# Hybrid decoder step on one core: the prompt's head norm moved into the samples' memory stage, and the samples' states loaded one stage earlier

## The chip, the cores and the metric

One Trainium2 chip, one of its cores. The metric is the device time of one execution in microseconds (us); lower is better. The profile has five engines: PE (TensorE; PEld is its weight load), DVE (VectorE), ACT (ScalarE), POOL (GpSimd) and SP (SyncE), from whose queue all DMAs here are issued.

## The reference, cut to what matters

One layer of a decoder runs on a prompt of 512 tokens (with 16 learned tokens ahead of it) and on 8 samples of 4 new tokens each. An input projection feeds 8 heads of differential attention and 4 heads of mLSTM, a matrix memory. Each head's output is normed, and the norms of all heads go into one output projection:

```
def rms_norm(x, g):
    y = xf * lax.rsqrt(jnp.mean(xf * xf, axis=-1, keepdims=True) + EPS)
    return (y * g.astype(jnp.float32)).astype(x.dtype)
...
    hn = rms_norm(h, g)                                  # mLSTM heads, 256 wide
    o = jax.nn.sigmoid(og.astype(jnp.float32)).reshape(B, T, N_HEADS_M, HEAD_DIM_M)
    return (hn * o).reshape(B, T, MLSTM_WIDTH)
...
    a = (rms_norm(a_heads, attn_out_norm) * (1.0 - lam_init)).reshape(B, T, ATT_WIDTH)
    x = x + jnp.concatenate([a, m_out], axis=-1) @ w_out
    hf = rms_norm(x, norm_ffn) @ w_up
    return x + jnp.square(jax.nn.relu(hf)) @ w_down
```

In an mLSTM head of a sample, the state C (256 by 256 for each of 8 samples and 4 heads, 8.4 MB together) is read from memory, used (`num = w_inter * (q @ C0) + s @ v`), updated (`C = w_c * C0 + k^T v`) and written back. The prompt's mLSTM begins with a state of zero.

## The kernel before, in words

The kernel is a row of stages. Each is a block in which the five engines run their own instruction lists and meet through semaphores; at its end all engines meet, and a second small block clears the stage's semaphores. So no work of one stage overlaps the next. The order is: input projection, attention of the prompt (`heads_and_attention`), conv and features (`mlstm_features`), the prompt's memory (`prompt_mlstm`), the samples' memory (`sample_mlstm`), attention of the samples over the paged cache (`decode_attention`), output projection (`finish_and_project`), MLP, output. All heads' outputs lie in one SBUF tensor, `mix` (128 partitions by 16 chunks of 128 features by 560 tokens: 528 of the prompt with the learned ones, then 32 of the samples).

`prompt_mlstm` loops over 4 heads with two sets of buffers. SP loads heads 0 and 1 (9 DMAs each, 2.5 MB, `load`, L1068), and then for each head waits for its state, stores it (L1087) and its normaliser (L1089: 256 elements of 4 bytes, each a run of its own), waits until the head's last output is placed and loads head h+2 into the freed buffers.

`sample_mlstm` first issues on SP, head by head, 7 small loads (L1277) and 8 loads of states (L1289, 256 KB each). TensorE does for each head h: `sums(h)` (L1426, 16 matmuls with the states of the 8 samples; the profile counts 32, since a float32 matmul shows as two instructions), one more for the new tokens (L1429), and then 16 outer products (L1458) into four PSUM banks in turn, which VectorE adds into the state one by one (L1379). VectorE also divides the head's output (`divide`, after `sums`), and prepares the next head in the middle of its additions (`weigh(h + 1)`). SP stores each new state as it is made (L1301). ScalarE is all but idle.

`finish_and_project` norms the heads and projects them. VectorE squares 16 chunks of 544 tokens (L2167), TensorE sums the squares over the partitions with one-hot weights (`gather`, L2231), ScalarE takes the sigmoid of the output gates `og` (L2119) and VectorE multiplies them in (L2173); then root (ScalarE, L2124) and reciprocal (VectorE, L2183) of all heads together; TensorE spreads the 12 rows of inverse roots over the partitions (`scatter`, L2241), and VectorE multiplies each chunk by it and the gain (L2194). ScalarE rounds the chunk to float32r (`mix_hi`, L2127) and VectorE makes the remainder (`mix_lo`, L2187). The weights of `w_out` come in 16 tiles of 1 MB and are split in the same way (L2094 on ScalarE, `leading`; L2139 on VectorE, `trailing`). A tile is 96 matmuls: two halves of 272 tokens, 16 chunks k, 3 passes (`exact_passes`, L69 to L71). Into the first tile's first half TensorE waits chunk by chunk for `mix_lo`. When all of `mix_lo` is made, `mix` is overwritten with the residual by one DMA of 4.35 MB (L2067), to which VectorE adds each tile's result (L2145). TensorE may begin tile n when tile n-2 has been added.

## Time and profile before

| | us |
|---|---|
| median of 3 runs | 3865.28 |
| lowest, highest | 3864.36, 3869.47 |
| the profiled execution: its time | 3864.66 |
| the same: its span | 3862.6 |
| TensorE busy | 3595.9 (93% of the span) |
| VectorE busy | 1808.7 (47%) |
| ScalarE busy | 1280.9 (33%) |
| the prompt's memory stage | 935.30 to 1042.37 |
| the samples' memory stage | 1042.37 to 1149.72 |
| output projection, before its first matmul with `w_out` | 2014.80 to 2080.80 |
| output projection, from there to its last matmul | 2080.80 to 2274.7 |

A stage begins with its first instruction or DMA issue. The busy share of TensorE is high in the projections and the MLP, and says little of the stages in this table: in the 66 us before the first matmul with `w_out` it is busy 37 us. Since all engines meet between stages, a stage counts with its own length.

### The profile page before, as it was taken

The numbers are of one execution on the slowest core, as the hardware profiler recorded it, in microseconds if no ns is written. First come the engines' busy times: TensorE is split into PE (matmuls) and PEld (weight loads), VectorE is DVE, ScalarE is ACT, GpSimd is POOL, SyncE is SP. The second block draws the span as 40 slices with busy tenths as digits, with TensorE's granted clock in tenths as the row PEclk, the third lists the DMA queues.
The fourth block names the chain that finished last, engine by engine and source line by source line (L and its number), as shares of the span: only waits on it lengthen the run. The fifth ranks groups of instructions, "written<-read, shape, count | busy, mean of one in ns | idle before, by whom it ended". The sixth has DMA issues, their size and how long they took to land. (4 is left out here: it accounts for less than half of the span.)

```text
span 3862.6 us, 65521 instructions
## 1 busy us (share of the span) xinstructions
PE 3595.9 (93%) x26234; PEld 3328.7 (86%) x26234; DVE 1808.7 (47%) x2749; ACT 1280.9 (33%) x1879; POOL 713.8 (18%) x436
## 2 busy tenths in 40 slices
PE   7999998866789999999977999999999999999998
PEld 7999996545658888888846999999999999999998
DVE  4222223764447777777765343333333333333333
ACT  3111111432107777777752232222222222222221
POOL 0000000000005888888870000000000000000000
PEclk9999999768869999999988999999999999999999
DMA  7443332115548899999964322222222222222221
GB/s 206 111 111 106 105 107 87 51 53 170 115 152 315 319 327 328 331 326 329 327 210 124 87 75 88 88 88 88 88 88 88 88 88 88 88 88 88 88 88 58
DMA packets 454169, 564.77 MB, mean 146 GB/s; under 512 B 39462, under 2 KB 330196, under 8 KB 453388
## 3 DMA queue, kind: packets, MB, share of 16 engines
q1 hardware_dynamic: 453932, 561.47, 45.3%
q8 instruction: 166, 2.72, 0.3%
q14 instruction: 71, 0.58, 0.0%
HBM read 514.93 MB, written 46.47 MB: 145 GB/s over the span
## 5 line engine op out<-in xcount | busy, mean ns | idle before, releaser
L1599 POOL TENSOR_TENSOR dc_vl<-dc_vpages,dc_vh 128x1024 fp32r<-128x1024 f32 x256 | 609.0, 2395 | 19.0 <-ACT dc_vh L1928 18.6
L69 PE MATMUL f_acc<-hidden_hi,ffn_lo 128*128 128x272 f32 x2048 | 591.7, 289 | 2.8 <-DVE mix_t L2353 2.8
L71 PE MATMUL f_acc<-xf_hi,ffn_hi 128*128 128x272 f32 x2048 | 594.1, 290 | 0.0
L71 PE MATMUL f_acc<-hidden_hi,ffn_hi 128*128 128x272 f32 x2048 | 592.9, 290 | 0.0
L69 PE MATMUL f_acc<-xf_hi,ffn_lo 128*128 128x272 f32 x2048 | 591.0, 289 | 1.0 <-DVE xf_lo L2375 0.4
L70 PE MATMUL f_acc<-hidden_lo,ffn_hi 128*128 128x272 f32 x2048 | 590.7, 288 | 0.0
L70 PE MATMUL f_acc<-xf_lo,ffn_hi 128*128 128x272 f32 x2048 | 588.5, 287 | 0.0
L69 PE MATMUL z_acc<-xn_hi,win_lo 128*128 128x280 f32 x1536 | 447.6, 291 | 1.1 <-DVE win_lo L302 1.1
L71 PE MATMUL z_acc<-xn_hi,win_hi 128*128 128x280 f32 x1536 | 448.5, 292 | 0.0
L2304 ACT ACTIVATE ffn_hi<-ffn_raw 128x2048 fp32r<-128x2048 f32 x127 | 242.3, 1908 | 619.4 <-PE f_acc L71 619.4
L70 PE MATMUL z_acc<-xn_lo,win_hi 128*128 128x280 f32 x1536 | 447.3, 291 | 0.0
L1770 DVE TENSOR_TENSOR dc_kl<-dc_pk,dc_kh 128x512 fp32r<-128x512 f32 x512 | 337.7, 681 | 151.9 <-ACT dc_kh L1928 151.4
L69 PEld LDWEIGHTS f_acc<-hidden_hi,ffn_lo 128*128 128x128 f32 x2048 | 384.5, 188 | 6.4 <-DVE mix_t L2353 6.4
L69 PEld LDWEIGHTS f_acc<-xf_hi,ffn_lo 128*128 128x128 f32 x2048 | 385.7, 188 | 4.3 <-DVE xf_lo L2375 3.6
L70 PEld LDWEIGHTS f_acc<-xf_lo,ffn_hi 128*128 128x128 f32 x2048 | 386.6, 189 | 0.0
L70 PEld LDWEIGHTS f_acc<-hidden_lo,ffn_hi 128*128 128x128 f32 x2048 | 386.0, 188 | 0.0
L71 PEld LDWEIGHTS f_acc<-xf_hi,ffn_hi 128*128 128x128 f32 x2048 | 385.4, 188 | 0.0
L71 PEld LDWEIGHTS f_acc<-hidden_hi,ffn_hi 128*128 128x128 f32 x2048 | 384.9, 188 | 0.0
L2358 DVE TENSOR_TENSOR ffn_lo<-ffn_raw,ffn_hi 128x2048 fp32r<-128x2048 f32 x127 | 291.2, 2293 | 150.8 <-ACT ffn_hi L2304 150.8
L2353 DVE TENSOR_TENSOR mix_t<-mix_t,f_acc 128x544 f32<-128x544 f32 x256 | 182.9, 720 | 362.1 <-PE f_acc L71 362.1
L1928 ACT ACTIVATE dc_kh<-dc_pk 128x512 fp32r<-128x512 f32 x512 | 278.4, 596 | 127.3 <-PE dc_pk L1627 126.3
L69 PEld LDWEIGHTS z_acc<-xn_hi,win_lo 128*128 128x128 f32 x1536 | 289.4, 188 | 1.3 <-DVE win_lo L302 1.3
(359 smaller groups left out, 6248.8 us busy)
## 6 DMA issues: line engine op xcount, KB each, us to landing
dc_kpages<-in_cache_k SPq DMA_DIRECT2D x256, 512.0 KB, 5.4
dc_vpages<-in_cache_v SPq DMA_DIRECT2D x256, 512.0 KB, 5.2
ffn_raw<-in_w_up SPq DMA_DIRECT2D x64, 1024.0 KB, 6.4
ffn_raw<-in_w_down SPq DMA_DIRECT2D x64, 1024.0 KB, 5.0
win_raw<-in_w_in SPq DMA_DIRECT2D x48, 1024.0 KB, 6.1
ffn_raw<-in_w_out SPq DMA_DIRECT2D x16, 1024.0 KB, 6.3
z_scratch<-z_out SPq DMA_DIRECT2D x48, 280.0 KB, 2.4
sm_c<-in_state_C SPq DMA_DIRECT2D x32, 256.0 KB, 4.5
```

What stands on the lines that cost most here:

```text
L69: nc.tensor.matmul(out, wlo, xhi, start=first, stop=False)
L70: nc.tensor.matmul(out, whi, xlo, start=False, stop=False)
L71: return nc.tensor.matmul(out, whi, xhi, start=False, stop=last)
L1599: G.tensor_tensor(vl[:, m % VBUF, :], vring[:, m % RING, :], vh[:, m % VBUF, :].bitcast(F32), ALU.subtract).then_inc(vlo, 1)
L1770: V.tensor_tensor(kl[:, k, hs, i * P:(i + 1) * P], pk[i][half][:, :].rearrange("p (h t) -> p h t", h=HH), kh[:, k, hs, i * P:(i + 1) * P]. ...
L1928: A = lambda out, x, **more: nc.scalar.activation(out, x, ACT.Copy, **more)
L2304: nc.scalar.activation(flow.hi[:, i % 2, :], flow.raw[:, i % G, :], ACT.Copy).then_inc(flow.hi_made, 1)
L2353: nc.vector.tensor_tensor(halves(xt[:, oc, :]), halves(xt[:, oc, :]), acc[2 + i % 2][:, :, 0:d.ohalf], ALU.add).then_inc(added, 1)
L2358: nc.vector.tensor_tensor(flow.lo[:, i % 2, :], flow.raw[:, i % G, :], flow.hi[:, i % 2, :].bitcast(F32), ALU.subtract).then_inc(flow.lo_m ...
```

## The change

Three things are done together.

- **States.** The buffers of the samples' states and their semaphores are made before `prompt_mlstm` (class `Early`, in a stage of its own around both), and the 32 loads of states are issued there, on SP, behind the loads of heads 0 and 1 and ahead of the first store.
- **Head norm of the prompt.** The norm and the output gate of the 512 prompt tokens move from `finish_and_project` into `sample_mlstm`: squares on ScalarE and 8 sums of squares (512 columns each) on TensorE behind each of the first two heads' outer products; behind head 1 the root, the reciprocal and the four gates; the 12 rows of inverse roots go to DRAM and come back as 12 broadcast loads, queued on SP behind the stores of head 1; behind head 2 VectorE multiplies 16 chunks. `num` has one PSUM bank in place of two, and the other is `mean`.
- **Output stage.** Only the 32 sample tokens are normed there, in one instruction where there were 16. The `w_out` tile 0 is loaded first. Both halves of `mix_hi` and `mix_lo` are made separately (`columns`): half 0 is all prompt tokens and its first 8 chunks are split at once, half 1 after the samples' norm. The residual comes in four DMAs, each when four chunks of half 1 have been split.

The functions not shown below are as before. The core of the diff:

```diff
+    def __init__(self, nc, ctx, d, sems):
+        self.states = [ctx.enter_context(nc.sbuf_tensor(f"sm_c0{h}", [P, d.nb, d.md // P, d.md + 1], F32))
+                       for h in range(d.hm)]
+        self.states_in = [sems(f"sm_c_in{h}") for h in range(d.hm)]
...
             for h in range(d.hm):
+                for b in range(d.nb):
+                    sp.dma_start(early.states[h][:, b, :, 0:d.md], a["state_C"][0, b, h].rearrange(
+                        "(e p) n -> p e n", p=P)).then_inc(early.states_in[h], 16)
...
         score = ps("sm_score", [P, 512])
-        num = [ps(f"sm_num{i}", [P, 512]) for i in range(2)]
+        num = ps("sm_num", [P, 512])
+        mean = ps("ph_mean", [P, 512])
...
             sp.dma_start(nrows[:, :], a["state_n"][0].rearrange("b h n -> (b h) n")).then_inc(states_in, 16)
             for h in range(d.hm):
                 load(sp, h)
-                load_states(sp, h)
+            for i in range(d.hm):
+                sp.dma_start(og[i][:, :, :], ogv[cog // E + i][:, :, N_META:TP]).then_inc(og_in[i], 16)
...
                                  c0[h][:, b, :, 0:MD]).then_inc(stored, 16)
+                if h == 1:
+                    sp.wait_ge(inv_made, 1)
+                    sp.dma_start(inv_dram, inv[:, :]).then_inc(inv_out, 16)
+                    sp.wait_ge(inv_out, 16)
+                    for i in range(NH):
...
+                dve.wait_ge(sigmoid_made, h + 1)
+                dve.wait_ge(squared, d.ha + (h + 1) * E)
+                x = prompt[:, d.ha + h * E:d.ha + (h + 1) * E, :]
+                V.tensor_tensor(x, x, og[h][:, :, :], ALU.mult).then_inc(gated, 1)
+            def invert():
+                dve.wait_ge(gathered, d.kc)
+                V.tensor_scalar(root[:, :], mean[0:NH, 0:S], EPS, None, ALU.add).then_inc(rooting, 1)
+                dve.wait_ge(rooted, 1)
...
+                    V.tensor_scalar(gains[:, 0:1], gains[:, 0:1], 1.0 - LAM_INIT, None, ALU.mult).then_inc(gated, 1)
+                    dve.wait_ge(gated, d.hm + 1)
+                gain = gains[:, 0:1] if n < d.ha else gains[:, 1 + (n - d.ha) % E:2 + (n - d.ha) % E]
+                V.scalar_tensor_tensor(prompt[:, n, :], prompt[:, n, :], gain, spread[:, head(n), :],
+                                       ALU.mult, ALU.mult).then_inc(normed, 1)
             for s in range(d.hm):
...
+                if h == 1:
+                    invert()
+                    for i in range(d.hm):
+                        gate(i)
                 dve.wait_ge(state_new, E * NB * (h + 1))
                 V.tensor_copy(nbh(ncols[:, :, :])[:, :, :, h], c0[h][:, :, :, MD]).then_inc(new_put, 1)
+                if h == d.hm - 2:
+                    for n in range(d.kc):
+                        norm(n)
             for e in range(E):
                 dve.wait_ge(new_turned, e + 1)
...
+                for n in part(h):
+                    if n >= 8:
+                        act.wait_ge(gathered, n - 7)
+                    nc.scalar.activation(sq[n % 8][:, :], prompt[:, n, :], ACT.Square).then_inc(squared, 1)
                 act.wait_ge(summed, h + 1)
...
                     raise_weights(h + 1)
+                if h == 1:
+                    for i in range(d.hm):
+                        act.wait_ge(og_in[i], 16)
+                        nc.scalar.activation(og[i][:, :, :], og[i][:, :, :], ACT.Sigmoid).then_inc(sigmoid_made, 1)
+                    act.wait_ge(rooting, 1)
+                    nc.scalar.activation(root[:, :], root[:, :], ACT.Sqrt).then_inc(rooted, 1)
...
                 pe.wait_ge(states_put, h + 2)
-                if h >= 2:
-                    pe.wait_ge(divided, h - 1)
+                if h:
...
                         scores(h + 1)
+                for n in part(h):
+                    pe.wait_ge(squared, n + 1)
+                    pe.wait_ge(gather_made, 3)
+                    x = head(n)
+                    nc.tensor.matmul(mean[0:NH, 0:S], gather[:, int(n >= d.ha), NH - 1 - x:2 * NH - 1 - x], sq[n % 8][:, :],
+                                     start=(n == 0), stop=(n == d.kc - 1)).then_inc(gathered, 1)
             pe.wait_ge(new_put, d.hm)
...
         def _(sp):
+            sp.dma_start(tile(flow.raw, 0), w[:, :, 0:P]).then_inc(flow.landed[0], 16)
+            sp.dma_start(og[:, :, :], ogv[:, :, d.tp:d.t]).then_inc(og_in, 16)
...
                 sp.dma_start(tile(flow.raw, j), w[:, :, j * P:(j + 1) * P]).then_inc(flow.landed[j], 16)
-            for h in range(2, d.hm):
-                sp.wait_ge(gated, (h - 1) * E)
-                sp.dma_start(og[:, h % 2, :, :], ogv[cog // E + h][:, :, N_META:d.t]).then_inc(og_in[h % 2], 16)
-            sp.wait_ge(lo_made, d.kc)
-            sp.dma_start(xt[:, :, :], x_dram.rearrange("(k p) t -> p k t", p=P)[:, :, N_META:d.t]).then_inc(residual_in, 16)
+            x = x_dram.rearrange("(k p) t -> p k t", p=P)[:, :, N_META:d.t]
+            for i in range(4):
+                rows = slice(i * QUAD, (i + 1) * QUAD)
+                sp.wait_ge(lo_made, N + (i + 1) * QUAD)
+                sp.dma_start(xt[:, rows, :], x[:, rows, :]).then_inc(residual_in, 16)
             with sp.Fori(0, N // GROUP - 1) as g:
...
-                act.wait_ge(og_in[h % 2], 16 * (h // 2 + 1))
-                nc.scalar.activation(og[:, h % 2, :, :], og[:, h % 2, :, :], ACT.Sigmoid).then_inc(sigmoid_made, 1)
...
+            for n in range(N // 2):
+                split(0, n)
+            act.wait_ge(og_in, 16)
...
             nc.scalar.activation(root[:, :], root[:, :], ACT.Sqrt).then_inc(rooted, 1)
-            for n in range(d.kc):
-                act.wait_ge(scaled, n + 1)
-                nc.scalar.activation(mhi[:, n, :], mix[:, n, :], ACT.Copy).then_inc(hi_made, 1)
+            act.wait_ge(flow.landed[0], 16)
+            leading(0)
+            for n in range(N // 2, N):
+                split(0, n)
+            act.wait_ge(scaled, 3)
+            for n in range(N):
+                split(1, n)
+                if n == N // 2:
+                    act.wait_ge(flow.landed[1], 16)
...
-                    dve.wait_ge(sigmoid_made, h + 1)
-                    dve.wait_ge(squared, i + 1)
-                    x = mix[:, d.ha + h * E:d.ha + (h + 1) * E, :]
-                    V.tensor_tensor(x, x, og[:, h % 2, :, :], ALU.mult).then_inc(gated, E)
-                if i in (9, 11):
-                    trailing(dve, (i - 9) // 2, (i - 9) // 2)
+            V.tensor_tensor(ssq[:, :, :], smp, smp, ALU.mult).then_inc(squared, 1)
...
+                trail(0, n)
             dve.wait_ge(gains_in, 32)
             V.tensor_scalar(gains[:, 0:1], gains[:, 0:1], 1.0 - LAM_INIT, None, ALU.mult).then_inc(gated, 1)
-            dve.wait_ge(gated, d.hm * E + 1)
-            dve.wait_ge(summed, d.kc)
-            V.tensor_scalar(two(root[:, :]), mean[0:NH, :, 0:d.ohalf], EPS, None, ALU.add).then_inc(rooting, 1)
+            dve.wait_ge(summed, 1)
+            V.tensor_scalar(root[:, :], means[0:NH, 0:TS], EPS, None, ALU.add).then_inc(rooting, 1)
+            dve.wait_ge(sigmoid_made, 1)
+            V.tensor_tensor(smp[:, d.ha:N, :], smp[:, d.ha:N, :], og[:, :, :], ALU.mult).then_inc(gated, 1)
...
-            def trail(n):
-                dve.wait_ge(hi_made, n + 1)
...
-                dve.wait_ge(spread_ready, h + 1)
-                V.scalar_tensor_tensor(two(mix[:, n, :]), two(mix[:, n, :]), gain, spread[h % 2][:, :, 0:d.ohalf],
+            V.reciprocal(inv[:, :], root[:, :]).then_inc(inverted, 1)
+            trailing(dve, 0, 0)
+            dve.wait_ge(gated, 2)
+            dve.wait_ge(spread_ready, 1)
+            rows = lambda lo, hi: spread[:, lo * TS:hi * TS].rearrange("p (h t) -> p h t", t=TS)
+            V.scalar_tensor_tensor(smp[:, 0:d.ha, :], smp[:, 0:d.ha, :], gains[:, 0:1], rows(0, d.ha),
+                                   ALU.mult, ALU.mult).then_inc(scaled, 1)
+            heads_m = smp[:, d.ha:N, :].rearrange("p (h e) t -> p e h t", e=E)
+            for e in range(E):
+                V.scalar_tensor_tensor(heads_m[:, e], heads_m[:, e], gains[:, 1 + e:2 + e], rows(d.ha, NH),
                                        ALU.mult, ALU.mult).then_inc(scaled, 1)
-                if n >= 1:
-                    trail(n - 1)
-            trail(d.kc - 1)
+            for n in range(N // 2, N):
+                trail(0, n)
+            for n in range(N):
+                trail(1, n)
+                if n == N // 2:
+                    trailing(dve, 1, 1)
             dve_group(dve, 0, True)
             with dve.Fori(1, N // GROUP) as g:
...
         def _(pe):
-            pe.wait_ge(consts, 6)
-            for i in range(d.kc):
-                n = d.ha + i if i < d.kc - d.ha else i - (d.kc - d.ha)
-                h = head(n)
-                pe.wait_ge(squared, i + 1)
-                for b in range(2):
-                    mm = nc.tensor.matmul(mean[0:NH, b, 0:d.ohalf], gather[:, int(n >= d.ha), NH - 1 - h:2 * NH - 1 - h],
-                                          sq[i % 2][:, b * d.ohalf:(b + 1) * d.ohalf], start=(i == 0),
-                                          stop=(i == d.kc - 1))
-                mm.then_inc(summed, 1)
+            pe.wait_ge(consts, 5)
+            pe.wait_ge(squared, 1)
+            for n in range(N):
+                x = head(n)
+                mm = nc.tensor.matmul(means[0:NH, 0:TS], gather[:, int(n >= d.ha), NH - 1 - x:2 * NH - 1 - x],
+                                      ssq[:, n, :], start=(n == 0), stop=(n == N - 1))
+            mm.then_inc(summed, 1)
             pe.wait_ge(inverted, 1)
             for h in range(NH):
-                if h >= 2:
-                    pe.wait_ge(scaled, h - 1 if h - 2 < d.ha else d.ha + (h - 1 - d.ha) * E)
-                for b in range(2):
-                    mm = nc.tensor.matmul(spread[h % 2][:, b, 0:d.ohalf], scatter[:, h, :],
-                                          inv[:, b * d.ohalf:(b + 1) * d.ohalf], start=True, stop=True)
...
-                sample_mlstm(nc, d, a, sems, c, qk_dram, kt_dram, vt_dram, g_dram, mix, c_sample, n_sample)
+            with ExitStack() as two, stage(nc) as early_sems:
+                early = Early(nc, two, d, early_sems)
+                with stage(nc) as sems:
+                    prompt_mlstm(nc, d, a, sems, c, qk_dram, kt_dram, vt_dram, g_dram, mix, c_prompt, n_prompt, early)
+                with stage(nc) as sems:
+                    sample_mlstm(nc, d, a, sems, c, z_dram, qk_dram, kt_dram, vt_dram, g_dram, inv_dram, mix, c_sample,
```

## Rows read from the trace of the kernel before

**Rows 1.** The page: its first line.
```profile
span 3862.6 us, 65521 instructions
```

**Rows 2.** Windows, output stage: length, PE, PEld, DVE, ACT, POOL, PEclk, DMA share, GB/s.
```profile
2014.80:2080.80 66.00, 37.16 (x112) 16.45 (x113) 41.34 (x51) 19.54 (x22) 3.76 (x6) 0.78 0.35 98
...
2094.00:2274.70 180.70, 180.70 (x1439) 180.55 (x1437) 54.67 (x45) 36.98 (x30) 0.00 (x0) 1.00 0.38 104
```

**Rows 3.** Timeline of that stage, PE and ACT: start us, us, what.
```profile
2080.80 0.81 PE L69 MATMUL o_acc<-mix_hi,ffn_lo 128*128 128x272 f32 x1
...
2093.92 1.92 ACT L2094 ACTIVATE ffn_hi<-ffn_raw 128x2048 fp32r<-128x2048 f32 x1 [8.76 <-PE o_acc L71]
```

**Rows 4.** Groups of instructions by line, the same stage.
```profile
L2194 DVE SCALAR_TENSOR_TENSOR mix_t<-mix_t,fh_gains,fh_spread 128x544 f32<-128x544 f32 x16 | 12.4, 775 | 3.3 <-PE fh_spread L2241 3.3
...
L2183 DVE RECIPROCAL fh_inv<-fh_root 12x544 f32<-12x544 f32 x1 | 3.5, 3541 | 0.7 <-ACT fh_root L2124 0.7
...
L2139 DVE TENSOR_TENSOR ffn_lo<-ffn_raw,ffn_hi 128x2048 fp32r<-128x2048 f32 x16 | 36.7, 2292 | 6.6 <-ACT ffn_hi L2094 6.6
...
L2094 ACT ACTIVATE ffn_hi<-ffn_raw 128x2048 fp32r<-128x2048 f32 x16 | 30.7, 1918 | 134.9 <-PE o_acc L71 129.0 <-DMA ffn_raw<-in_w_out 5.9
...
L2127 ACT ACTIVATE mix_hi<-mix_t 128x544 fp32r<-128x544 f32 x16 | 10.5, 658 | 17.2 <-DVE mix_t L2194 17.2
```

**Rows 5.** Timeline of ScalarE, the same stage: one table load.
```profile
2040.58 1.28 ACT L2124 ACT_TABLE_LOAD   x1
```

**Rows 6.** DMA issues: KB each, us to landing (second: 1042.3 to 1046).
```profile
ffn_raw<-in_w_out SPq DMA_DIRECT2D x16, 1024.0 KB, 6.3
...
sm_qk<-qk_scratch SPq DMA_DIRECT2D x1, 64.0 KB, 2.0
```

**Rows 7.** Timeline of VectorE at the first addition of the residual.
```profile
2099.51 0.72 DVE L2145 TENSOR_TENSOR mix_t<-mix_t,o_acc 128x544 f32<-128x544 f32 x1 [13.59 <-DMA mix_t<-xt_scratch]
```

**Rows 8.** Timeline of TensorE in the samples' memory stage.
```profile
1047.66 0.42 PE L1413 MATMUL sm_score<-sm_qk 128*32 128x32 f32 x4 [2.55 <-DMA sm_src<-g_scratch]
...
1056.17 9.73 PE L1426 MATMUL sm_num<-sm_c,sm_qpad 128*32 128x257 f32 x32 [8.08 <-DMA sm_c<-in_state_C]
...
1078.59 8.79 PE L1426 MATMUL sm_num<-sm_c,sm_qpad 128*32 128x257 f32 x32
...
1100.08 9.97 PE L1426 MATMUL sm_num<-sm_c,sm_qpad 128*32 128x257 f32 x32
```

**Rows 9.** Windows of the same stage, columns as in Rows 2.
```profile
1056.20:1061.50 5.30, 5.30 (x13) 2.23 (x14) 0.00 (x0) 0.00 (x0) 0.00 (x0) 0.50 1.06 337
...
1071.90:1082.00 10.10, 8.22 (x19) 4.23 (x18) 6.10 (x19) 0.00 (x0) 0.00 (x0) 0.50 1.00 325
```

**Rows 10.** Timeline of TensorE: the sums of squares of the output stage.
```profile
2052.03 3.91 PE L2231 MATMUL fh_spread<-fh_sq,fh_gather 128*12 128x272 f32 x16 [1.47 <-DVE fh_sq L2167]
```

**Rows 11.** Timeline of the prompt's memory stage: SP's queue, then VectorE.
```profile
967.38 0.47 SPq L1089 DMA_DIRECT2D out<-ml_state  x1
...
971.49 0.37 SPq L1068 DMA_DIRECT2D ml_qk<-qk_scratch  x1
...
993.08 1.51 DVE L1194 TENSOR_SCALAR ml_w<-ml_negtop,ml_src 112x528 f32<-112x528 f32 x5
```

**Rows 12.** Windows of the prompt's stage; the last is of the samples'.
```profile
936.00:954.50 18.50, 7.71 (x23) 5.16 (x24) 4.54 (x14) 2.69 (x7) 0.00 (x0) 0.56 1.02 289
...
972.00:978.00 6.00, 4.68 (x29) 3.49 (x27) 5.61 (x18) 2.27 (x7) 0.00 (x0) 1.00 0.74 44
...
978.00:988.00 10.00, 9.89 (x68) 8.97 (x67) 6.60 (x19) 0.92 (x3) 0.00 (x0) 1.00 1.01 242
...
1058.00:1061.00 3.00, 3.00 (x9) 1.23 (x8) 0.00 (x0) 0.00 (x0) 0.00 (x0) 0.50 1.06 365
```

**Rows 13.** Timeline at a stage boundary: last instruction, first of the next.
```profile
2011.70 0.20 ACT L1928 ACTIVATE mix_t<-dc_pscore 128x32 f32<-128x32 f32 x1 [13.18 <-PE dc_pscore L1720]
...
2014.80 0.34 SPq L2055 DMA_DIRECT2D fh_gains<-in_attn_out_norm  x1
```

128 lines of the change are left out of this document (76 added, 52 removed).

## The prediction

> **What bounds the kernel now.** I read the page first: the span is 3862.6 us [rows 1]. Since all engines meet between stages, no average over the span prices this change; three stretches do. The windows of the output stage give the first: 66.0 us pass before its first matmul with `w_out`, with TensorE busy 37 of them and VectorE 41, neither full [rows 2]. The PE timeline dates that matmul at 2080.80 [rows 3]. From there TensorE is busy all the time: 180.7 us after 2094.0, 0.1256 us per matmul, so 12.06 for a tile of 96. The first tile ends at 2093.92, where ScalarE is released [rows 3]. Second, the samples' memory stage: TensorE idles 8.08 us for the states' DMA before `sums(0)`, then the heads follow each other 22.4 and 21.5 us apart, with 8.8 to 10 us of `sums` in each, in which VectorE has nothing [rows 8]. Third, the prompt's memory stage hides its loads, and the question there is by how much.
>
> **Output stage.** Removed: squares, gates, reciprocal over 544 columns, and 16 chunk norms with their splits, ahead of the projection. What releases the first matmul now is the weights' split behind the samples' norm. From the stage's start at 2014.80:
> - `w_out` tile 0, issued first, lands after about 6.3 us, as such tiles do [rows 6]: 2021.1. The samples' gates are issued next, 1024 runs of 128 bytes; 512 such runs landed 2.0 us after issue on a free queue [rows 6], so about a microsecond behind the tile: 2022.0. ScalarE's eight first splits are done by then (272 columns, half of 0.66 us each or a little more [rows 4], 3 us).
> - ScalarE: the table load for the sigmoid (1.28 [rows 5]) fits before 2022.0; sigmoid of 256 columns 0.4, table load for the root 1.28, root 0.2, then `leading(0)` 1.92 [rows 4]: 2025.8.
> - VectorE: `trailing(0)` 2.29 [rows 4]: 2028.1. TensorE starts there instead of at 2080.80.
>
> TensorE will have done only 28 small matmul pairs before and starts at the half clock. In the samples' stage a burst after idling ran at 0.50 for 5.3 us [rows 9]; that much at half clock costs 2.65 us. VectorE must keep ahead: after 2028.1 three small products (1.0), then 24 half-chunk remainders of about 0.38 with `trailing(1)` (2.29) between. It finishes chunk 9 of half 1 at 2038.5, and TensorE reaches it at 2028.1 + 2.65 + 6.03 + 3.4 = 2040.2; after that both go at 0.38. No stall, by 1.7 us. So tile 0 ends at 2028.1 + 12.06 + 2.65 = 2042.8 instead of 2093.92: **-51.1 us**. The residual (4.35 MB, 13.6 us with its wait before [rows 7]) is now asked for from about 2034 to 2041 in quarters and is there by 2048; then addition 0.72 and `trailing(2)` 2.29, 2051, and TensorE wants tile 2 at 2042.8 + 12.06 = 2054.9. Hidden, by 4 us. Bounds: everything at its earliest (gates together with the tile, warm clock) -54.5; gates landing 4 us later and 3 us of stalls -44.
>
> **Samples' memory stage.** (a) With the states there, `sums(0)` follows the scores at 1047.66 + 0.42, say 1048.3 instead of 1056.17 [rows 8]: -7.9. (b) 8 sums of squares behind head 0's outer products. TensorE executes in order, so `sums(1)` comes after them, and VectorE has nothing to do meanwhile: all of it is on the path. At full clock 16 instructions of 272 columns took 3.91 [rows 10], so 512 columns are 0.46 each and 16 of them 7.4; at half clock 14.8. The stretch in which they start ran at 0.50 until 1082.0 [rows 9], 3.4 us into them: I take 3.4 + 16 x 0.46 - 1.7 = 9.0. `sums(1)` then runs at full clock, 16 pairs of 257 columns, 32 x 0.23 (0.244 x 257/272) = 7.4 where it took 8.79: net +7.6. (c) The same behind head 1, 7.4 to 9, take 8.0; but here VectorE's chain to head 2 decides: root's addition 0.7, root 0.66, reciprocal 3.3 (3.54 for 544 columns), four gates of 1024 columns at 1.2 (half of a 2048-column remainder [rows 4]) 4.8, hand-overs 0.3: 9.8 behind the last sum, against 9.97 + 0.8 for `sums(2)` and its division before [rows 8]: 8.0 + 9.8 - 10.8 = +7.0. (d) Sixteen norms of 512 columns, 775 x 512/544 = 730 ns [rows 4], 11.7 with 0.4 around, beside `sums(3)` of about 10 and 0.6: +1.5. Their inputs: the inverse roots leave some 4.8 us after the last sum, are in DRAM 2 us later, 12 issues of 0.5 follow, and 3 MB need 11 us at 289 GB/s [rows 12]: 18 to 20 us, where VectorE wants them after 9.8 + 13 = 23. Squares (5 us), sigmoids and table loads lie on an idle ScalarE; one bank for `num` costs nothing, since `divide` is over 12 us before the next `sums`. Sum: **+8.2 us**. Bounds: +4 (both groups at full clock, norms under `sums(3)`) and +20 (both at half clock).
>
> **Prompt's memory stage.** The 32 state loads are issued on SP in 16 us from 948.6, behind the first 5.3 MB, which end at 954.5 at 289 GB/s [rows 12]. State loads alone ran at 365 GB/s [rows 12]: 8.4 MB take 23.0 us, to 977.5. Queued behind them are the first store of the state, the 4-byte store of the normaliser, and the load of head 2. Before, that store was issued at 967.38 and the load at 971.49 [rows 11], and though nothing else was in the queue the load crawled at 44 GB/s from 972 to 978 and went at 242 only then [rows 12]: the small store holds the queue for some 10 us. Head 2 is wanted at 993.08 [rows 11], and the load was in by about 991 to 992 (the window 978 to 988 moved 2.4 of its 2.5 MB, the rest trickled), so 1 to 2 us are spare. If the store now begins at 978 instead of 967.9, everything behind it moves by 10, and head 2 starts 8 to 9 us late; load 3 suffers the same shift and adds 1. I take **+9**. Below: if store and states overlap in the queue, the 2.5 MB land by 988 and nothing is lost: 0. Above: states at 289 GB/s, +14.
>
> [...]
>
> **Boundary.** `Early` has a block of its own that clears 4 semaphores. Two such blocks and their meetings took 2014.80 - 2011.90 = 2.9 us [rows 13]; one more, nearly empty: **+1** (0.5 to 1.5). Decoding, MLP and output keep their work.
>
> **Sum.** -51.1 + 8.2 + 9 + 1 = -32.9. The profiled execution (3864.66, 2.1 above its span) becomes 3831.8; the median is 0.6 above it, so 3832.
>
> **The rivals.**
> - *States hidden.* The prompt's stage keeps its length. For it: the states' bytes fit into the empty queue between 954.5 and 978. Against: the crawl. -42, 3823.
> - *TensorE's extra sums at half clock and late broadcasts.* For it: half of the samples' stage ran at 0.50. Samples +20, prompt +12: -18, 3847.
> - *Output stage gives back.* The four residual DMAs queue ahead of `w_out` tile 4 and behind each other, or VectorE's splits keep TensorE waiting in half 1: up to 10 us more, -23, 3842. Against: 4 and 1.7 us of margin above, though the latter is small.
> - *Slower: the broadcasts.* Each of 12 loads reads one row of 2 KB 128 times. If such loads go one after another at the 44 GB/s of the crawl rather than at 289, 3 MB take 70 us, 50 more than is free; norm 0 waits and with it VectorE and the fourth head: +17, 3882. It decides from 60 us for the twelve, 5 us each. Against: the first 5.3 MB held four broadcasts and ran at 289 GB/s overall [rows 12].
>
> **How the numbers follow.** Forecast (within 5 us of 3832) 0.45, hidden states 0.17, half clock 0.18, output stage gives back 0.14, broadcasts 0.04, something else that costs 30 us 0.02. The range 3819 to 3851 leaves out 1 in 10 below and above together with the slower cases; the forecast's own range is 3826 to 3839. 0.2% (7.7 us) is about what a measurement of this kernel can tell from no change. Faster holds the first four cases, 0.94; within 0.2% the last, 0.02; slower the broadcasts, 0.04.
>
> **What would show it.** First matmul with `w_out` 13 to 14 us after its stage's first issue (66 before); half clock in its first 5 us; no wait of tile 2. In the samples' stage `sums(0)` 6 us after the stage's start, its length up by 8.2 (the 7.9 of waiting already taken off); VectorE's first norm not waiting for a DMA. In the prompt's stage, VectorE waiting some 9 us for `ml_src` ahead of head 2. The prediction is wrong if that wait is absent, if the sums of squares run at half clock throughout, or if VectorE waits for `ph_spread`.

## The result

The changed kernel took 3833.8 us (median of 4 runs, 3826.6 to 3834.7) beside 3865.2 for the kernel before (4 runs, 3864.4 to 3869.5): a ratio of 0.9913, 95% interval 0.9901 to 0.9925. Forecast were 3832 and a range of 3819 to 3851. A later set with the same kernel gave 3834.6 (5 runs) and 0.9921 (0.9908 to 0.9935).

The profiled execution took 3832.93 us. The first line of its page, which answers to [rows 1]:

```profile
span 3831.2 us, 65582 instructions
```

All engines meet between stages, so the difference of the two spans, -31.4, can be booked stage by stage. A stage runs from SP's first DMA issue in it to the first of the next stage; the output stage is cut where ScalarE is released by the end of tile 0.

| | before | after | moved | forecast |
|---|---|---|---|---|
| all before the prompt's memory stage | 935.30 | 933.88 | -1.4 | 0 |
| prompt's memory stage | 107.07 | 114.45 | +7.4 | +9 |
| samples' memory stage | 107.35 | 117.71 | +10.4 | +8.2, and +1 for the block |
| decoding | 865.08 | 869.41 | +4.3 | 0 |
| output stage up to the end of tile 0 | 79.12 | 28.09 | -51.0 | -51.1 |
| the rest | 1768.68 | 1767.66 | -1.0 | 0 |

**Output stage.** Windows of the kernel after (columns as in [rows 2]): from the first issue to the first matmul with `w_out`, then tile 0, then the tiles behind it.

```profile
2035.45:2049.79 14.34, 7.13 (x56) 6.90 (x56) 8.43 (x15) 10.24 (x21) 3.45 (x5) 0.50 0.96 242
2049.79:2063.54 13.75, 13.75 (x100) 13.75 (x100) 11.65 (x28) 7.04 (x18) 0.00 (x0) 0.89 0.78 237
2063.54:2243.00 179.46, 179.46 (x1431) 179.46 (x1430) 54.67 (x45) 37.05 (x30) 0.00 (x0) 1.00 0.39 105
```

14.34 us pass instead of 66.0, tile 0 has no gap in it, and behind it TensorE is busy for all of 179.46 us, at 0.1254 us per matmul: nothing is given back. What stands on the way to the first matmul is shown by the timelines of ScalarE, VectorE and TensorE in the kernel after:

```profile
2042.15 0.42 ACT L2212 ACTIVATE fh_og<-fh_og 128x256 f32<-128x256 f32 x1 [2.71 <-DMA fh_og<-z_scratch]
...
2044.02 1.89 ACT L2183 ACTIVATE ffn_hi<-ffn_raw 128x2048 fp32r<-128x2048 f32 x1
...
2063.54 1.92 ACT L2183 ACTIVATE ffn_hi<-ffn_raw 128x2048 fp32r<-128x2048 f32 x1 [5.48 <-PE o_acc L71]
...
2075.59 1.92 ACT L2183 ACTIVATE ffn_hi<-ffn_raw 128x2048 fp32r<-128x2048 f32 x1 [4.06 <-PE o_acc L71]
```
```profile
2045.94 2.29 DVE L2236 TENSOR_TENSOR ffn_lo<-ffn_raw,ffn_hi 128x2048 fp32r<-128x2048 f32 x1 [1.46 <-ACT ffn_hi L2183]
```
```profile
2044.54 5.33 PE L2330 MATMUL fh_spread<-fh_inv,fh_scatter 12*128 12x32 f32 x24 [3.44 <-DVE fh_inv L2276]
2049.79 0.59 PE L69 MATMUL o_acc<-mix_hi,ffn_lo 128*128 128x272 f32 x1
```

The weights' remainder (`trailing(0)`, L2236) is done at 2048.23, 12.8 us after the stage's start; the forecast had 13.3. But TensorE starts only at 2049.79. Its 24 small products with `fh_scatter`, which run at the half clock of the first window (0.50), end no earlier. So the last thing to end is another instruction than in the forecast, 1.6 us behind it. Tile 0 ends at 2063.54 and the next at 2075.59, 12.05 later, so tile 2 does not wait. The residual comes late, as the timeline of VectorE shows (kernel after), but it is hidden: the addition and `trailing(2)` behind it are done at 2073.04, 2.5 us before TensorE wants tile 2 (the forecast had 4).

```profile
2070.11 0.72 DVE L2242 TENSOR_TENSOR mix_t<-mix_t,o_acc 128x544 f32<-128x544 f32 x1 [8.47 <-DMA mix_t<-xt_scratch]
```

**Samples' memory stage.** The timeline of TensorE, kernel after; rows of `sm_num<-sm_c` answer to [rows 8], those of L1550 are the sums of squares:

```profile
1053.65 0.42 PE L1495 MATMUL sm_score<-sm_qk 128*32 128x32 f32 x4 [2.31 <-DMA sm_src<-g_scratch]
1054.37 9.60 PE L1508 MATMUL sm_num<-sm_c,sm_qpad 128*32 128x257 f32 x32 [0.30 <-DVE sm_c L1376]
...
1076.66 8.63 PE L1550 MATMUL ph_mean<-ph_sq,ph_gather 128*12 128x512 f32 x16
1085.12 7.12 PE L1508 MATMUL sm_num<-sm_c,sm_qpad 128*32 128x257 f32 x32
...
1104.93 9.84 PE L1550 MATMUL ph_mean<-ph_sq,ph_gather 128*12 128x512 f32 x16
1114.62 7.12 PE L1508 MATMUL sm_num<-sm_c,sm_qpad 128*32 128x257 f32 x32
...
1135.67 9.91 PE L1508 MATMUL sm_num<-sm_c,sm_qpad 128*32 128x257 f32 x32
...
1148.54 10.62 PE L1540 MATMUL sm_acc<-sm_v,sm_kw 32*128 32x257 f32 x24
```

The wait of 8.08 us for the states is gone: `sums(0)` starts 6.04 us after the stage's first issue (1048.33) where it started 13.80 after. From there the heads follow each other at 30.75, 29.50 and 21.05 us, where they were 22.4, 21.5 and 24.4 apart: +8.3, +8.0, -3.4 at the starts of `sums`. By the divisions, with which VectorE takes up each head (16.4, 44.7, 75.7 and 98.8 us after the stage's start, where it was 24.3, 45.8, 68.5 and 92.6), it is +6.8, +8.3 and -1.0. The last row matters for the account: head 3's 24 outer products took 10.62 us, and 7.35 in the timeline of the kernel before:

```profile
1136.63 7.35 PE L1458 MATMUL sm_acc<-sm_v,sm_kw 32*128 32x257 f32 x24
```

The timeline of VectorE between the last sum of squares and head 2's division, and at the norms:

```profile
1114.82 0.68 DVE L1412 TENSOR_SCALAR ph_root<-ph_mean 12x512 f32<-12x512 f32 x1 [9.29 <-PE ph_mean L1550]
1116.19 3.34 DVE L1414 RECIPROCAL ph_inv<-ph_root 12x512 f32<-12x512 f32 x1 [0.69 <-ACT ph_root L1486]
1119.46 4.55 DVE L1408 TENSOR_TENSOR mix_t<-mix_t,ph_og 128x1024 f32<-128x1024 f32 x4
...
1124.38 0.47 DVE L1397 TENSOR_SCALAR sm_out<-sm_num,sm_mag 32x256 f32<-32x256 f32 x1
...
1136.57 10.69 DVE L1423 SCALAR_TENSOR_TENSOR mix_t<-mix_t,ph_gains,ph_spread 128x512 f32<-128x512 f32 x16
```

The chain of 9.8 us that was forecast behind the last sum (from 1114.77) took 9.25 to the division's first instruction at 1124.02. The norms begin at 1136.57 without a wait: the twelve broadcasts, issued from 1121.09 to 1127.26, were there.

**Prompt's memory stage.** SP's queue, then VectorE and TensorE at head 2, in the timeline of the kernel after; these answer to [rows 11]:

```profile
947.27 25.82 SPq L1096 DMA_DIRECT2D sm_c<-in_state_C  x32
973.13 0.66 SPq L1101 DMA_DIRECT2D out<-ml_state  x1
973.84 0.67 SPq L1103 DMA_DIRECT2D out<-ml_state  x1
974.55 0.66 SPq L1078 DMA_DIRECT2D ml_qk<-qk_scratch  x1
```
```profile
996.39 1.53 DVE L1208 TENSOR_SCALAR ml_w<-ml_negtop,ml_src 112x528 f32<-112x528 f32 x5 [4.95 <-DMA ml_src<-g_scratch]
```
```profile
996.41 5.88 PE L1125 MATMUL ml_score<-ml_qk 128*112 128x264 f32 x12 [6.63 <-DMA ml_src<-g_scratch]
```

The windows of the same stretch (to set beside [rows 12]):

```profile
972.00:978.00 6.00, 5.27 (x38) 4.66 (x39) 5.61 (x16) 0.55 (x3) 0.00 (x0) 1.00 1.09 349
978.00:984.00 6.00, 6.00 (x47) 5.63 (x46) 4.86 (x15) 0.53 (x2) 0.00 (x0) 1.00 1.06 186
984.00:990.00 6.00, 5.79 (x42) 5.32 (x40) 0.09 (x1) 0.95 (x3) 0.00 (x0) 1.00 1.01 217
```

The crawl of the kernel before (44 GB/s from 972 to 978) does not come back here: the states move at 349 GB/s until 978, and the load behind them at 186 and 217. VectorE waits 4.95 us for `ml_src` before head 2, TensorE 6.63. And TensorE, which had idled for these 6.63 us, computes head 2's first scores in 5.88 us. The same products took 3.37 in the timeline of the kernel before:

```profile
991.34 3.37 PE L1111 MATMUL ml_score<-ml_qk 128*112 128x264 f32 x12
```

The granted clock was 1.00 under that row, and 0.50 from 993.0 to 999.0 and 0.64 from there to 1002.3 in the kernel after. The wait and these slower products (the cold start, below) make the stage longer. The forecast had a wait of 8 to 9 us and no cold start.

### The profile page after: what moved, and what is told of

It is laid out like the page before. It is cut to its first block and busy times, and to the rows that moved or that the text cites. A ratio compares the mean times of both kernels' runs of the same rounds, so it can differ in the third digit from the quotient of the medians.

```text
span 3831.2 us, 65582 instructions
## 1 busy us (share of the span) xinstructions
PE 3588.0 (94%) x26210; PEld 3326.5 (87%) x26210; DVE 1801.5 (47%) x2757; ACT 1293.2 (34%) x1916; POOL 713.4 (19%) x438
```

## The experiments

All twelve were timed beside the kernel before on the same chip. e1 to e4 came in one set, e5 to e8 in a second, f1 to f4 in a third; the kernel before took 3863.7, 3864.9 and 3865.2 us in them. The ratio, which is formed within a set, is the safer figure for a comparison across sets.

| kernel | median us (runs) | ratio, 95% interval | prompt's / samples' / decoding | head 3's outer products |
|---|---|---|---|---|
| before (first profile) | 3865.2 (4) | | 107.1 / 107.4 / 865.1 | 7.35 |
| after (first profile) | 3833.8 (4) | 0.9913 [0.9901, 0.9925] | 114.5 / 117.7 / 869.4 | 10.62 |
| e1 | 3864.7 (10) | 1.0004 [0.9994, 1.0014] | 114.9 / 97.3 / 868.3 | 8.23 |
| e2 | 3831.9 (4) | 0.9919 [0.9902, 0.9935] | 106.8 / 124.1 / 866.6 | 8.12 |
| e3 | 3827.1 (4) | 0.9907 [0.9891, 0.9924] | 111.8 / 114.7 / 866.5 | 7.96 |
| e4 | 3823.1 (4) | 0.9892 [0.9875, 0.9908] | 106.6 / 116.9 / 870.9 | 9.68 |
| e5 | 3825.5 (4) | 0.9896 [0.9879, 0.9912] | 114.9 / 111.1 / 868.8 | 9.12 |
| e6 | 3828.5 (4) | 0.9905 [0.9889, 0.9922] | 114.8 / 116.4 / 866.2 | 10.02 |
| e7 | 3830.7 (4) | 0.9915 [0.9898, 0.9931] | 114.5 / 115.9 / 867.9 | 8.03 |
| e8 | 3824.0 (4) | 0.9894 [0.9878, 0.9911] | 106.9 / 115.2 / 869.2 | 10.61 |
| f1, the changed kernel again | 3834.6 (5) | 0.9921 [0.9908, 0.9935] | 115.1 / 114.6 / 866.5 | 8.01 |
| f4, e4 again | 3824.2 (4) | 0.9895 [0.9880, 0.9911] | 106.9 / 116.2 / 868.1 | 8.05 |
| f2 | 3849.3 (5) | 0.9953 [0.9940, 0.9967] | 107.7 / 139.8 / 868.0 | 10.61 |
| f3 | 3866.8 (1) | | 107.9 / 105.4 / 868.0 | 8.30 |

The three stage lengths are differences of first issues in each kernel's timeline; the last column is its row for the outer products of head 3.

**e1: the early states alone.** The kernel before, plus class `Early` and the 32 loads behind the loads of heads 0 and 1; nothing else of the change.

```diff
+            for h in range(d.hm):
+                for b in range(d.nb):
+                    sp.dma_start(early.states[h][:, b, :, 0:d.md], a["state_C"][0, b, h].rearrange(
+                        "(e p) n -> p e n", p=P)).then_inc(early.states_in[h], 16)
...
-                load_states(sp, h)
```

> The kernel before, with one part of the change alone: the 32 loads of states are issued in the prompt's memory stage behind the first two heads' loads. Theory A (the small 4-byte store and the loads behind the states arrive late, and the third head waits): the prompt's stage is 7 us longer, the samples' stage 8 us shorter by its wait for states and 1 us longer by the extra block; in total 3865 plus 0, within 2 us. Rival B (the states are hidden in an empty queue): the prompt's stage keeps its 107.1 us, and the kernel takes 3858.

The time did not move (1.0004). The prompt's stage is 7.9 us longer and the samples' 10.0 shorter. Of these 10.0, 7.8 are the wait for the states. The rest lies in the later heads, where the same code also differs by 2 us between two executions (107.4 in before, 105.4 in f3). The timeline of VectorE in e1 has the wait in its new place:

```profile
998.23 1.53 DVE L1207 TENSOR_SCALAR ml_w<-ml_negtop,ml_src 112x528 f32<-112x528 f32 x5 [6.31 <-DMA ml_src<-g_scratch]
```

So in this kernel the early loads only carry the wait from one stage into another.

**e2: the change without the early states.** Its loads issued in `sample_mlstm` again, behind each head's small loads.

```diff
-            for h in range(d.hm):
-                for b in range(d.nb):
-                    sp.dma_start(early.states[h][:, b, :, 0:d.md], ...
...
             for h in range(d.hm):
                 load(sp, h)
+                for b in range(NB):
+                    sp.dma_start(c0[h][:, b, :, 0:MD], a["state_C"][0, b, h].rearrange(
+                        "(e p) n -> p e n", p=P)).then_inc(c_in[h], 16)
```

> The changed kernel with the loads of states back in the samples' stage, each head's 8 behind its 7 small loads; all else is kept. Theory A: the prompt's stage falls back from 114.5 to 107.1 us, and the samples' first product with the states starts 13.8 us after the stage's start instead of 6.0, so that the two cancel: 3833 to 3835, as the changed kernel. Rival B (the early loads are worth their 8 us of waiting): 3841.

3831.9, as quick as the change. The prompt's stage has its old length (106.8), and the samples' is 6.3 us longer than in the first profile of after, 9.4 longer than in f1. The whole gain of the change is that of the moved norm together with the new order of the output stage (`w_out` tile 0 first, halves split apart, residual in quarters). No run takes these two from each other.

**e3: the small store behind the next load.** In the changed kernel the store of the normaliser (L1103, 256 values of 4 bytes, two for each partition) goes behind the load of head h+2.

```diff
-                sp.dma_start(n_prompt[0, 0, h].rearrange("(e p) -> p e", p=P), state[s][:, :, d.md],
-                             allow_slow_non_contiguous=True).then_inc(stored[s], 16)
                 if h + 2 < d.hm:
                     sp.wait_ge(placed, NT * (h + 1))
                     load(sp, h + 2, s)
+                sp.dma_start(n_prompt[0, 0, h].rearrange("(e p) -> p e", p=P), state[s][:, :, d.md],
+                             allow_slow_non_contiguous=True).then_inc(stored[s], 16)
```

> The changed kernel with one order changed on SP's queue: in the prompt's stage the store of the normaliser (256 runs of 4 bytes) is issued behind the load of head h+2 instead of ahead of it. The bytes stay the same. Theory A (the small store holds the queue some 10 us, behind the states): the third head waits 2 us at most instead of 5, its matmuls keep the full clock, and the prompt's stage is 5 to 7 us shorter than in the changed kernel: 3827. Rival B (it is the bytes of the states alone that delay the load): the load's landing does not move, and the time is that of the changed kernel, 3833.

The timeline of VectorE in e3 at head 2:

```profile
992.75 1.52 DVE L1208 TENSOR_SCALAR ml_w<-ml_negtop,ml_src 112x528 f32<-112x528 f32 x5 [2.45 <-DMA ml_src<-g_scratch]
```

The wait is 2.45 us instead of 4.95, and the stage 2.6 to 3.2 shorter than in the two profiles of after. So the small store's place accounts for half of the wait. The other half goes only when the states' loads go (e2 and e4). The median of 3827.1 lies lower by more than that, but the interval of its ratio overlaps that of the change, and only the 2.5 us are tied to a row.

**e4 and f4: only head 0's states early.** The other 24 loads go out in the samples' stage, behind each head's small loads.

```diff
-            for h in range(d.hm):
+            for h in range(1):
                 for b in range(d.nb):
                     sp.dma_start(early.states[h][:, b, :, 0:d.md], ...
```

> The changed kernel with only head 0's 8 loads of states (2.1 MB) early; the other 24 are issued in the samples' stage, behind each head's small loads. Theory A: 2.1 MB are through 6 us after the first heads' loads, before the first store is issued; the prompt's stage falls back to 107.1 us, and the samples' first product still starts 6 us after the stage's start: 7 us less than the changed kernel, 3826. Rival B (24 loads, 6.3 MB, in the samples' stage delay head 1, or push the output gates and stores behind them): head 1 waits, and the gain is under 3 us.

> Only head 0's eight state loads early, once more, beside the changed kernel in the same set: 8 us less than it (3824 to 3825) by the theory; under 5 us less by the rival.

SP's queue in e4's timeline:

```profile
947.47 7.20 SPq L1096 DMA_DIRECT2D sm_c<-in_state_C  x8
965.57 0.38 SPq L1101 DMA_DIRECT2D out<-ml_state  x1
```

Eight loads leave SP in 7.20 us, and the first store waits for its data, not for the queue. No engine waits for a DMA at head 2, the prompt's stage takes 106.6 and 106.9 us, and `sums(0)` still starts 6.0 and 7.6 us after the samples' stage begins; `sums(1)` follows the sums of squares without a wait, so heads 1 to 3 need no earlier load. 3823.1 and 3824.2: the best version of the study, measured twice. In the third set it stands beside the changed kernel, 3824.2 against 3834.6.

**f1: the changed kernel again.**

> The changed kernel itself, unchanged, timed beside the next two. Theory: the 8 to 10 us by which the version with only head 0's states early was quicker are the wait and the cold start at head 2 of the prompt's memory stage, so this one gives 3832 to 3834 and that one 3823 to 3825 in the same set. Rival: part of the difference lay between chips; then they stand less than 5 us apart. Decoding, whose code is the same in all kernels, has taken 865.1 to 870.9 us so far; the theory that this is variation from run to run expects a figure in that range that need not be the 869.4 of the first profile, the rival that the change itself made it longer expects 869 again.

3834.6, and 10.4 us behind f4 in the same set (9.0 by the means): the difference is not one between chips. The profiles show 8.1 in the prompt's stage (115.05 against 106.93). They can't book the rest: the profiled execution of f1 is the fastest of its five (3826.8, the others 3834.5 and more), and it lies only 4.3 us above that of f4. Decoding took 866.5 here and 869.4 in the first profile of the same kernel. Over the 14 traces, whose code there is the same, it ranges from 865.1 to 870.9 with a mean of 867.8, and it falls into no order by kernel; the first profile of before has the lowest of them. The +4.3 of the account is therefore most likely chance in one pair of executions. So is most of the 3.3 us at head 3: its outer products take 8.01 here, 10.62 there.

**e5: fewer sums of squares.** Seven of the eight matmul pairs behind head 0's outer products are left out, so the means lack these sums. The first pair waits for all eight squares and reports for all eight.

```diff
                 for n in part(h):
+                    if 1 <= n < 8:
+                        continue
...
```

> The changed kernel without seven of the eight matmuls (14 of 16 instructions) that sum the squares behind head 0: the means of attention heads 1 to 7 lack their sums. Theory A (they stand on the path, since VectorE has nothing to do meanwhile and sums(1) is queued behind them): 14 instructions of 0.46 to 0.9 us go, and sums(1) falls back to a partly half clock: 5 to 7 us less than the changed kernel, 3828. Rival B (TensorE has slack there, or the clock gives it all back): within 2 us of the changed kernel.

The group takes 1.88 us in place of 8.6 (first profile) or 8.4 (f1). The samples' stage is 111.1 us and the time 3825.5. In the timeline `sums(1)` starts 30.21 us after the stage's start instead of 36.79 (first profile) or 36.17 (f1): the group lies on the path with its whole length. Seven pairs gave back 6.0 to 6.6 us, 0.9 us a pair, and nothing covers them.

**e6: the gates on GpSimd.** The four products with the sigmoids leave VectorE's chain to head 2.

```diff
-                V.tensor_tensor(x, x, og[h][:, :, :], ALU.mult).then_inc(gated, 1)
+                nc.gpsimd.tensor_tensor(x, x, og[h][:, :, :], ALU.mult).then_inc(gated, 1)
```

> The changed kernel with the four gate products of the prompt on GpSimd instead of VectorE. Theory A (VectorE's chain behind head 1 is 1.4 us longer than sums(2), so the gates are nearly all covered): divide(2) comes 1.4 us earlier, and the kernel gains 1 to 1.5 us: 3832. Rival B (the whole 4.6 us of the gates are on the path): 3829. Rival C (GpSimd and VectorE slow each other, or GpSimd is too late for the norms): slower than the changed kernel.

GpSimd needs 9.26 us for what VectorE did in 4.55, but it does them while the sums of squares run:

```profile
1100.72 9.26 POOL L1367 TENSOR_TENSOR mix_t<-mix_t,ph_og 128x1024 f32<-128x1024 f32 x4 [51.93 <-ACT ph_og L1485]
```

Head 2's `sm_out` follows the last sum by 8.1 us instead of 9.6. The limit is then TensorE's `sums(2)` (7.12) with the magnitude and the division behind it, so that 1.5 of the 4.55 us come out. The interval of the ratio doesn't set it apart from the change.

**e7: the output stage in another order.** The samples' gates loaded ahead of `w_out` tile 0, sigmoid and root ahead of ScalarE's eight splits, VectorE's eight remainders behind the reciprocal, the means ahead of the wait for `fh_scatter`. The first parts of the edit:

```diff
-            sp.dma_start(tile(flow.raw, 0), w[:, :, 0:P]).then_inc(flow.landed[0], 16)
             sp.dma_start(og[:, :, :], ogv[:, :, d.tp:d.t]).then_inc(og_in, 16)
+            sp.dma_start(tile(flow.raw, 0), w[:, :, 0:P]).then_inc(flow.landed[0], 16)
...
-            for n in range(N // 2):
-                split(0, n)
             act.wait_ge(og_in, 16)
...
+            for n in range(N // 2):
+                split(0, n)
...
```

> The changed kernel with another order at the start of the output stage: the samples' gates are loaded ahead of the first tile of w_out, their sigmoid and root come ahead of the eight splits, and the sums of squares wait only for the gather weights, not for the scatter weights too. Theory A (the first matmul with w_out waits for TensorE's own 12 small spreading matmuls, which run at half clock for 5.3 us because the inverse root is late): it starts 11.2 us after the stage's start instead of 14.3, and the kernel gains 3 us: 3830. Rival B (the tile's landing and its split on ScalarE and VectorE set the start): it starts later than now, since the tile is asked for later, and nothing is gained.

The gates land after 2.4 us instead of 6.2, and the sigmoid starts 2.5 us after the stage's first issue instead of 6.7. Yet the first matmul with `w_out` comes 14.50 us after that issue, no earlier than in the changed kernel (14.34 and 14.49 in its two profiles). The timelines of VectorE and TensorE in e7 say what took the place of the wait:

```profile
2040.67 0.15 DVE L2268 TENSOR_SCALAR fh_gains<-fh_gains 128x1 f32<-128x1 f32 x1 [6.02 <-DMA fh_gains<-in_mlstm_out_norm]
```
```profile
2047.91 0.60 PE L69 MATMUL o_acc<-mix_hi,ffn_lo 128*128 128x272 f32 x1 [0.98 <-DVE ffn_lo L2236]
```

The addition to `fh_root` is queued behind the first of these instructions, which waits for 1.5 KB of gains until 7.3 us after the first issue. ScalarE's eight splits now lie between the root and `leading(0)`. TensorE waits 0.98 us for VectorE's remainder of the weights at the end, where it was its own small products that ended last. Moving one of these chains brought up another, and nothing was gained.

**e8: e4, e6 and e7 together.**

> The changed kernel with three edits together: only head 0's states early, the gates on GpSimd, and the new order in the output stage. If all three theories hold, the gains add: 7 + 1.4 + 3 = 11 us less than the changed kernel, 3822. If they overlap in the clock or the queue, 5 to 8 us.

3824.0, the same as e4. Its profile has the 106.9 of the prompt's stage; what e6 and e7 were hoped to add does not show. It would be within what decoding and head 3's outer products (10.61) vary by.

**f2: operands exchanged.** On top of e4 the squares are the weights and one column of 1/width passes through. The means lie with tokens on the partitions, and root and reciprocal work on 48 columns.

```diff
-                    nc.tensor.matmul(mean[0:NH, 0:S], gather[:, int(n >= d.ha), NH - 1 - x:2 * NH - 1 - x], sq[n % 8][:, :],
-                                     start=(n == 0), stop=(n == d.kc - 1)).then_inc(gathered, 1)
+                            mm = nc.tensor.matmul(mean[:, x * J + j:x * J + j + 1], sq[n % 8][:, j * P:(j + 1) * P],
+                                                  gather[:, int(n >= d.ha), NH - 1:NH],
+                                                  start=(n == chunks[0]), stop=(n == chunks[-1]))
```

> Head 0's states alone early, and the sums of squares with the operands exchanged: the squares are the weights (128x128, four for each chunk) and one column of 1/width passes through, so that the means come out with tokens on the partitions, 48 columns instead of 12 rows of 512; the root and the reciprocal work on 48 columns, one transposition turns them back for the store. 32 matmuls (64 instructions) of one column for each group in place of 8 (16 instructions) of 512. Theory A, time goes by the columns that pass through: a group takes 4 us or less where it took 8.6 and 9.8, head 1 comes 4 to 5 us earlier, head 2 another 5 to 6 (the reciprocal's 3.3 us no longer stand in its way either): 3812 to 3815. Theory B, with one column each instruction costs its weights' load, 0.13 us as for the 80-column products of the prompt's stage (9 in 1.17 us): 8.3 us a group, nothing gained there, 1 to 2 us from the reciprocal: 3822.

Neither theory was right: at 3849.3 it is slower than the changed kernel. Theory B was the nearer one: an instruction of one column took 0.216 us, where one of 512 columns took 0.54 in the change (8.63 us for 16, granted clock 0.81); but it is 0.216 and not 0.13. Timeline of TensorE at the first group, then the windows of both groups, in f2:

```profile
1071.94 13.81 PE L1564 MATMUL ph_mean<-ph_gather,ph_sq 128*128 128x1 f32 x64
1085.68 9.61 PE L1517 MATMUL sm_num<-sm_c,sm_qpad 128*32 128x257 f32 x32
```
```profile
1071.94:1085.68 13.74, 13.74 (x65) 13.73 (x64) 0.66 (x2) 4.41 (x7) 0.00 (x0) 0.50 0.91 319
1107.98:1121.72 13.74, 13.74 (x65) 13.73 (x64) 0.48 (x1) 0.00 (x0) 0.00 (x0) 0.50 0.10 35
```

0.216 us for each instruction of one column, with PEld busy throughout and the granted clock at 0.50 in both groups. The next `sums` ran at a granted clock of 0.74 and 0.82 and took 9.61 and 8.66 us, where e4 had 7.12 both times, at 1.00. The reciprocal did shrink, from 3.34 to 0.45 us. A second loss is of this version's own making: the copy of the turned inverses waits in ScalarE's order behind head 3's weights, the store goes out at 1136.93, and VectorE waits 7.17 us for `ph_spread` before the norms:

```profile
1151.48 0.15 DVE L1426 TENSOR_SCALAR ph_gains<-ph_gains 128x1 f32<-128x1 f32 x1 [7.17 <-DMA ph_spread<-inv_scratch]
```

This is the wait that the rival "broadcasts" spoke of. Here it comes from a late store, 15.2 us after the last sum where the change has 4.8. The broadcasts landed as quickly as there (a median of 5.6 us after their issue, 5.2 in the change).

**f3: the small store late in the kernel before.** The same edit as e3, on the kernel before.

> The kernel before, with the store of the normaliser (256 values of 4 bytes, two for each partition) issued behind the loads of the head after next instead of ahead of them. Theory: this small store is what held the queue, and the 44 GB/s of the windows from 966 to 978 us become 250 or more, head 2's load is in by about 980, and the time is that of before (3865 within 3), since head 2 is only wanted at 993. Rival: the load crawls for its own sake (its many short rows); then the windows stay at 44 GB/s.

Windows of f3, against the 44 GB/s of 972 to 978 in [rows 12]:

```profile
972.00:978.00 6.00, 4.57 (x30) 3.57 (x29) 5.58 (x18) 1.65 (x6) 0.00 (x0) 1.00 1.03 298
978.00:984.00 6.00, 6.00 (x51) 5.76 (x51) 4.86 (x15) 0.53 (x2) 0.00 (x0) 1.00 0.66 148
```

And DMA issues from 964 to 996 us (KB each, median us to landing), first of the kernel before, then of f3:

```profile
ml_qk<-qk_scratch SPq DMA_DIRECT2D x2, 1056.0 KB, 11.2
...
ml_src<-g_scratch SPq DMA_DIRECT2D x1, 0.3 KB, 8.8
```
```profile
ml_qk<-qk_scratch SPq DMA_DIRECT2D x2, 1056.0 KB, 5.3
...
out<-ml_state SPq DMA_DIRECT2D x1, 1.0 KB, 12.7
```

The load moves at 298 GB/s as soon as it is issued (at 970.87), lands in half the time, and no crawl follows it: finer windows show 275 GB/s from 978 to 980, 167 to 982 and 1 from 982 to 984. So the 44 GB/s were not the load's own rate, but that of a large load behind the small store. The store itself is slow in either place: it lands 12.7 us after its issue here, and 9.9 (median of two) in the kernel before. Why it holds up the load, no run shows. The time did not change (3866.8, one run), since TensorE takes up head 2 only at 990.7.

## Why the prediction was right, point by point

- **Output stage, -51.1: measured -51.0**, but two errors cancelled. The weights' remainder was ready 0.5 us earlier than forecast, while TensorE was held 1.6 us longer by its own small products at half clock, which the forecast's path left out. Against that, tile 0 took 13.75 instead of 14.7, since the cold start cost 1.7 us (granted clock 0.89 over the tile) and not 2.65. That is partly luck: with the same code tile 0 took 14.46 in f1, and between 13.7 and 15.1 over all profiles with this output stage, so the cold start cost 1.7 to 3.0. In f1 the row stands at -50.2. The residual was hidden, and no tile waited.
- **States there at `sums(0)`, -7.9: measured -7.8** (13.80 to 6.04 after the stage's start).
- **First group of sums, +7.6: +6.8** by the division of head 1. The group took 8.63 where 9.0 stood and `sums(1)` 7.12 where 7.4 stood. e5 shows it on the path.
- **Second group and VectorE's chain, +7.0: +8.3.** The chain was right (9.25 for 9.8). The group was mis-sized: 8.0 was taken and it was 9.84. Its window, 1104.93 to 1114.62, shows a granted clock of 0.71, and that of the first group, 1076.66 to 1085.12, one of 0.81. Which of the two groups is the slower one changes: in e4 the first took 9.84 and the second 8.75. Together they took 18.0 to 18.6 us in all nine profiles that have both, where the forecast had 17.0.
- **Norms beside `sums(3)`, +1.5: -1.0.** They took 10.69 for 11.7. Head 2's other work, from its division to the norms, took 2.0 us less than in the kernel before (granted clock 0.65 over 1124 to 1136, against 0.59 over 1110 to 1124.5). The forecast had no term for that. The last head then took 3.0 us more at half clock (0.50). The other traces show this to vary, from 7.4 to 10.6 for the same 24 products.
- **Prompt's stage, +9: measured +7.4 to +8.0** (114.45 and 115.05 in its two profiles, 114.92 in e1). The mechanism held: e3 and e4 take parts of the queue's load away, and the wait shrinks to 2.45 and to nothing. Its parts were wrong, and they cancelled. SP needed 25.8 us to issue the 32 loads, not 16. The small store was issued at 973.84 and not at 978, and no crawl followed it, so head 2's last load left SP 6.3 us later than before and not 10. The wait was 4.95 us, not 8 to 9. Head 3 had none, where +1 stood. And 2.5 us came from TensorE's cold start after the wait (first scores in 5.88 us and not 3.37), which the forecast left out. That head 2's load comes behind the states and the small store ahead of it was the author's estimate, and the +9 rests on it: no run shows in what order the queue's transfers are written or reported. The runs show times: head 2's `ml_qk` landed 11.1 us after its issue in the kernel before and 5.4 in f3, where no small store is ahead of it, and the wait fell from 4.95 us to 2.45 in e3. The forecast's 10 us for the small store were too much at head 2: e3 found 2.5.
- **The block, +1: +1.1** (5.14 us from the samples' last issue to the next stage, 4.00 before), but the number was met by luck. e1 has the same extra block and shows 4.23, so the block costs 0.2. The samples' stage of the changed kernel has 16 semaphores more to clear than that of e1, and f2, with two more again, shows 5.25. The 0.91 us between 4.23 and 5.14 make 0.06 for each of the 16, an estimate, and the 0.11 of f2 for two agree with it.
- **Decoding, 0:** right as far as 14 traces can tell, though this pair of profiles shows +4.3.
- **The sum.** The four terms of the forecast make -32.9, and the same rows measure -33.3. The closeness hides +1.2 in the samples' row (with the block) and -1.6 in the prompt's. The remaining +1.9 is decoding and the rows that were forecast at 0. Since the same kernel's rows differ by 3 us between two profiles, a hit within 2 us is in part luck. The mechanism of each large term is what the runs bear out.
- **The rivals.** "States hidden" and "output stage gives back" fell. Half clock was there in parts: 0.81 and 0.71 in the two groups, not throughout. The twelve broadcasts landed 3.2 to 7.0 us after their issue, and no engine waited for them.
- **The signs.** The first matmul with `w_out` came 14.34 us after its stage's first issue (13 to 14 were named), `sums(0)` 6.04, and VectorE did not wait for `ph_spread`. The wait for `ml_src` was there, but about half as long as named.

What stays open: why head 3's outer products ran at a granted clock of 0.50 in one execution of the changed kernel (10.62 us) and at 0.67 in another (8.01 us, f1); why two of the changed kernel's nine executions took 3826.7 and the others 3833 to 3837; and why e3's median lies lower than its 2.5 us at head 2 explain.

## What to carry to other kernels

An early load was worth something here only where the queue ahead of its consumer had room for it: e1 moved 8.4 MB out of one stage into another and moved the wait with them (one stage 7.9 us longer, the other 10.0 shorter), while the 2.1 MB that the first consumer needs cost nothing (e4: 106.6 us for the prompt's stage, 107.1 before). Ask for each prefetch how much of it must be early, and what is queued behind it.

When a long chain ahead of a saturated TensorE is moved into a stage where TensorE has gaps only while another engine works, count the whole of its matmuls on the path, as e5 shows (0.9 us for each of seven pairs), and take the gain as the difference of two serial times. Near the end of such a chain several waits can end within a microsecond or two, as here, and removing one of them (e7) uncovers the next.
